# Transposing 64 rows in place of 128 for the half-filled expert blocks of a mixture-of-experts encoder layer

## The reference

```python
def expert_block(args):
    xb, e = args
    gt = jnp.minimum(xb @ w_gate[e] + b_gate[e], SWIGLU_LIMIT)
    up = jnp.clip(xb @ w_up[e] + b_up[e], -SWIGLU_LIMIT, SWIGLU_LIMIT)
    hdn = (up + 1.0) * (gt * jax.nn.sigmoid(SWIGLU_ALPHA * gt))
    return hdn @ w_down[e] + b_down[e]
...
out = jax.ops.segment_sum(y * gate, tok_pad, num_segments=T)
return rmsnorm(h + out, g_final)
```

## Time and profile before

| | |
|---|---|
| time, three runs | 1344.82, 1348.51 (median), 1349.32 us |
| profiled execution | 1343.44 us, of which the span of its instructions is 1341.7 us |
| TensorE busy | 1270.3 us (95%) |
| VectorE busy | 1230.4 us (92%) |
| ScalarE busy | 969.7 us (72%) |
| moved by DMA | 473.31 MB, 353 GB/s over the span |
| granted TensorE clock, mean | 0.981 |

### The profile page before, as it was taken

How to read it: one execution, slowest core, us unless ns; L and a number is a source line. 1 busy time by engine, 2 the same in 40 slices (tenths; PEclk the granted TensorE clock), 3 DMA queues, 4 the chain that set the end, 5 groups by cost and what they waited for, 6 DMA issues and landing times.

```text
span 1341.7 us, 17612 instructions
## 1 busy us (share of the span) xinstructions
PE 1270.3 (95%) x5771; PEld 1012.1 (75%) x5771; DVE 1230.4 (92%) x1014; ACT 969.7 (72%) x784; POOL 174.0 (13%) x165
## 2 busy tenths in 40 slices
PE   4998889878999999999999999999999999999997
PEld 3876767756878777787877777778787777777775
DVE  6798966699999999999999999999999999999998
ACT  3241665438797979797888888887979787879762
POOL 3010000012020101010101101020101010101243
PEclk9998989979999999999999999999999999999998
DMA  8964401489999999999999999999999999999985
GB/s 286 386 183 127 157 1 38 154 312 417 383 400 414 411 419 410 420 409 420 409 421 409 419 409 420 408 422 409 410 419 411 418 411 419 413 418 422 413 319 166
DMA packets 85574, 473.31 MB, mean 353 GB/s; under 512 B 11899, under 2 KB 12198, under 8 KB 36390
## 3 DMA queue, kind: packets, MB, share of 16 engines
q1 hardware_dynamic: 73838, 437.07, 81.0%
q0 software_dynamic: 6560, 18.90, 4.6%
q10 hardware_dynamic: 5144, 16.93, 3.3%
HBM read 447.72 MB, written 29.33 MB: 356 GB/s over the span
## 4 chain that ended last, share of the span: by engine, by line
PE 67%; DVE 14%; DMA 7%; ACT 6%; issue 3%; SPq 1%; ACTq 1%; POOL 0%; DVEq 0%
PE pair L1938 14%; PE pair L1939 13%; PE pair L1940 13%; DMA w_raw<-in_w_up 6%; PE pair L1954 5%; PE pair L1955 5%; DVE w_low L1285 5%; ACT w_high L831 3%; DVE area_m L1135 3%; PE pair L1925 2%; PE pair L1973 2%; PE pair L1952 1%; PE pair L1716 1%; PE pair L1717 1%; PE pair L1718 1%
## 5 line engine op out<-in xcount | busy, mean ns | idle before, releaser
L1285 DVE TENSOR_TENSOR w_low<-w_raw,w_high 128x2048 fp32r<-128x2048 f32 x380 | 838.4, 2247 | 40.9 <-ACT w_high L831 39.7
L831 ACT CAST w_high<-w_raw 128x2048 fp32r<-128x2048 f32 x380 | 702.9, 1878 | 170.4 <-PE pair L1940 117.1
L1938 PE MATMUL pair<-w_high,xT_high 128*128 128x512 f32 x528 | 211.4, 400 | 0.0
L1939 PE MATMUL pair<-w_low,xT_high 128*128 128x512 f32 x528 | 206.7, 392 | 0.0
L1940 PE MATMUL pair<-w_high,xT_low 128*128 128x512 f32 x528 | 206.1, 390 | 0.0
L1954 PE MATMUL pair<-w_high,xS 128*128 128x512 f32 x450 | 183.3, 407 | 0.1
L1955 PE MATMUL pair<-w_low,xS 128*128 128x512 f32 x450 | 175.8, 391 | 0.0
L1938 PEld LDWEIGHTS pair<-w_high,xT_high 128*128 128x128 f32 x528 | 99.2, 188 | 31.9 <-issue 11.4
L1940 PEld LDWEIGHTS pair<-w_high,xT_low 128*128 128x128 f32 x528 | 99.2, 188 | 21.5
L1939 PEld LDWEIGHTS pair<-w_low,xT_high 128*128 128x128 f32 x528 | 99.2, 188 | 19.1
L1938 PE MATMUL pair<-w_high,hT_high 128*128 128x512 f32 x256 | 102.0, 399 | 10.9 <-DVE w_low L1285 10.9
(11 more groups left out here) (355 smaller groups left out, 1793.5 us busy)
## 6 DMA issues: line engine op xcount, KB each, us to landing
w_raw<-in_w_gate SPq DMA_DIRECT2D x128, 1024.0 KB, 15.4
w_raw<-in_w_up SPq DMA_DIRECT2D x128, 1024.0 KB, 16.7
w_raw<-in_w_down SPq DMA_DIRECT2D x128, 1024.0 KB, 16.6
ring<-in_w_in SPq DMA_DIRECT2D x5, 2048.0 KB, 17.8
y_rows<-area_t SPq DMA_DIRECT2D x1, 8704.0 KB, 37.0
y_rows<-area_m ACTq DMA_DIRECT2D x15, 512.0 KB, 7.8
ring<-in_w_out SPq DMA_DIRECT2D x2, 2048.0 KB, 8.0
y_rows<-area_t SPq DMA_DIRECT2D x1, 3840.0 KB, 12.5
```

Of the source, the lines that this page charges most:

```text
L831: s.copy(w_high[:, i % HIGH_RING, raw:], w_raw[i][:, raw:]).then_inc(high_ready, 1)
L1285: v.tensor_tensor(w_low[i][:, raw:], w_raw[i][:, raw:], w_high[:, i % HIGH_RING, raw:].bitcast(F32), ALU.subtract).then_inc(low_ready, 1)
L1938: t.matmul(to[half], tok_high, hi, start=(opens and kk == 0), stop=False)
L1939: t.matmul(to[half], tok_high, lo, start=False, stop=False)
```

## The change

`transpose_x` and `transpose_h` get a parameter `first_row`. With 64, the first transpose of the set is as before and the other seven take the rows 64 to 127 alone: 64 x 128 stationary, 64 moving columns, written to the columns 64 to 127 of each 128. It is given for the x and the h of the small blocks 1, 3, ..., 29. That is 15 sets of x and 15 of h, so 210 instructions. All else, with the readers of the results, stays as it is.

```diff
-            def transpose_x(b):
+            def transpose_x(b, first_row=0):
                 pe.wait_ge(xg_loaded, 16 * (b + 1))
                 for k in range(KD):
-                    last = t.transpose(bank[6 + k // 4][:, (k % 4) * CAP:(k % 4 + 1) * CAP], xg[0:CAP, k::KD],
-                                       ident[0:CAP, 0:CAP])
+                    r = first_row if k else 0
+                    last = t.transpose(bank[6 + k // 4][:, (k % 4) * CAP + r:(k % 4 + 1) * CAP], xg[r:CAP, k::KD],
+                                       ident[r:CAP, r:CAP])
                 last.then_inc(xg_transposed, 1)
...
-            def transpose_h(b):
+            def transpose_h(b, first_row=0):
                 pe.wait_ge(h_tok_ready, b + 1)
                 for k in range(KD):
-                    last = t.transpose(bank[6 + k // 4][:, (k % 4) * CAP:(k % 4 + 1) * CAP], h_tok[:, k::KD],
-                                       ident[0:CAP, 0:CAP])
+                    r = first_row if k else 0
+                    last = t.transpose(bank[6 + k // 4][:, (k % 4) * CAP + r:(k % 4 + 1) * CAP], h_tok[r:, k::KD],
+                                       ident[r:CAP, r:CAP])
                 last.then_inc(h_transposed, 1)
...
-            def pe_odd(j):
+            def pe_odd(j, next_from=SMALL):
                 base = PIECES * j + 8
-                gate(j + 1, base, turn=j)
+                gate(j + 1, base, turn=j, turn_from=SMALL)
                 up(j + 1, base + UP)
                 pe.wait_ge(hT_low_ready, j + 1)
-                transpose_x(j + 2)
+                transpose_x(j + 2, next_from)
                 down(j, base + DOWN, small=True)
...
-            up(0, UP, high=x0T_high, low=x0T_low, between=lambda: transpose_x(1))
+            up(0, UP, high=x0T_high, low=x0T_low, between=lambda: transpose_x(1, SMALL))
...
-            pe_odd(N_EXPERTS - 3)
+            pe_odd(N_EXPERTS - 3, next_from=0)
```

More of the change, by code:

```diff
@@ L1975, in _, with gate @@
             G_TO, U_TO, D_TO = ([bank[i][0:CAP, :], bank[i + 1][0:CAP, :]] for i in (0, 2, 4))
-            def gate(b, base, turn=None, high=xT_high, low=xT_low, between=None, fold_down=None, small=False):
+            def gate(b, base, turn=None, high=xT_high, low=xT_low, between=None, fold_down=None, small=False, turn_from=0):
                 pe.wait_ge(sel_in_ready, b + 1)
@@ L1994, in gate @@
                     if i == 1 and turn is not None:
-                        transpose_h(turn)
+                        transpose_h(turn, turn_from)
                     if i == 1 and between is not None:
```

## The result

The changed kernel takes 1350.62 us (median of 12 runs, 1348.37 to 1356.17), the kernel before 1345.80 us in its 12 runs (1343.40 to 1349.89). The ratio is 1.0042, with a 95% interval of 1.0027 to 1.0057: slower by 0.4%, a little more than what can be told from no change.

What follows compares the result with a forecast made beforehand. TensorE bounds early pairs, weight transfers late ones. 28 sets at 0.28 us add 7.8, hidden by 8.8 to spare in a median run; 1348.5 plus 0.3 for the last set and 0.5 for meeting lines gives 1349.3 us, range 1345 to 1353.5.

Steps and rivals of the forecast that it cites:

- The bound: Experts' pairs of passes: TensorE sets the pace until the prefetch is used up near 957 us, then weight transfers do.
- TensorE's line: Pace of the experts' passes if TensorE's work alone set it: 63.23 us a pair.
- the transfers' line: Pace that weight loads allow the experts' passes: one pair in 64.2 us, taking over near 957 us.
- What a set costs: Eight transposes of a small block's x or h: 0.88 us before, 1.15 to 1.16 changed, so +0.28 us.
- The sign that the prediction gave: In the profile after, "issue" idle on PEld at L1918 and L1925, 0.1 to 0.2 us twice a set.
- The time to spare in the profiled execution: At the experts' last copy TensorE is 3.7 us ahead of transfers, hiding that much of 7.8 us added.
- To the median: Lays the 5.1 us from profiled execution to median to the transfer rate, giving TensorE 8.8 us to spare.
- the prediction's first rival: Spread of run times is not the transfers'; only 3.7 us spare in every run, so 1352.9 us, +0.33%; chance 0.25.
- The 0.5 us that it added for two lines that meet: In late pairs, TensorE and transfers within a microsecond wait now for one, now the other: about 0.5 us more.
- That a set costs nothing more: 64-row loads 0.063 us apart, or no drain for half-size transposes; time stays 1348.5 to 1348.6 us; chance 0.18.
- that the visit costs 0.41: Switching to 64 rows and back costs 0.41 us a set or above: 1351.6 us, or 1356.7; chance 0.10.
- the side on which fewer moving columns pay: Halved moving columns shorten transposes by 0.19 us a set and transfers only echo TensorE: 1342.9 us; chance 0.05.

Runs made afterwards that it cites:

- every second transpose: In each of the 30 sets, transposes k = 1, 3, 5, 7 take 64 rows and the others 128; against the kernel before, ratio 1.0254.
- x sets alone: Only the 15 x sets have seven 64-row transposes, h sets as in the kernel before; against that kernel, ratio 1.0007.

## Why the prediction was right and where it was wrong

**The bound: right.** TensorE's line and the transfers' line are in both profiles of before, with the same handover; taking TensorE's work away moved the handover forward and not the end. In the changed kernel the chain was to show no w_up transfer, TensorE's extra wait of late pairs was to be gone, and landing times were to rise by half a microsecond a pair. There is no such transfer, the idle time of the late pair is 63.90 - 63.50 = 0.4 us where it was 64.32 - 62.89 = 1.4, and landing times go from 9.7 to 15.5 us over 11 pairs.

**What a set costs: right in mechanism, a term too small.** The way in was put at 0.29 us from matmul to matmul and is 0.31 (0.20 to the load, 0.11 from there), the way out at 0.26 and is 0.26. Most of what was off is the middle, six distances put at 0.10 us and read off a single pair of loads; they are 0.108. Together +0.34 and not +0.28 a set; the pairs show 0.70 for two. 28 sets make 28 x 0.35 = 9.8 us in place of 7.8. The sentence on the Trainium skill's page "TensorE: Matmul & The Clock Gate", section "LDWEIGHTS (loading the stationary operand)", would have given 0.107 for the distance and +0.32, nearer to what was measured. That a load's time goes by the columns and not by the rows agrees as far as the rows go: loads of 64 rows and 128 columns follow each other by 0.108 us, those of 128 rows by 0.11; no run here changes the columns. The drain that the Trainium skill's page "TensorEngine Tiling (Array Packing)" names under "Key Properties" fits what is paid for, here 0.20 us in and about 0.15 us out; the traces show loads that begin late, not what TensorE does meanwhile. The sign that the prediction gave, "issue" idle of 0.1 to 0.2 us twice a set, stands once a set, on the way in, with 0.24; the way out shows only in the distance of the loads.

**The time to spare in the profiled execution: right.** With the measured cost, 9.8 - 3.7 = 6.1 us were to be added between the first and the last copy. It is (1220.6 - 323.8) - (1213.6 - 322.8) = 6.0. The set behind them, 0.3, is not seen: from there to the end are 127.8 us (1348.4 - 1220.6) against 128.1. The x set of block 1 costs nothing, as said: with four visits in it, in the kernel with every second transpose, the first copy is at 322.8 as before. The 3.7 itself is 3.8 from start to start, since the row at 387.95 of the earlier trace rows is the last 0.90 us of a copy that takes 1.00.

**The step "To the median": wrong, and it decided the forecast's side.** It laid the 5.1 us between the profiled execution and the median of three runs to the rate of the transfers, and so gave TensorE 8.8 us to spare in a median run. The profiles put the spread in the attention, ahead of the experts, where it goes with TensorE's clock, and it shifts both lines; 3.7 us are all there is to spare. This was the prediction's first rival, held at 0.25, and it is the one that happened: with the set's cost as forecast it gives 4.4 us or 0.33%, with the measured one 28 x 0.35 - 3.7 + 0.35 = 6.4 us or 0.48%, beside a measured 0.42% (0.27 to 0.57). That the forecast's absolute time is near is partly luck: its base of 1348.5 us was 2.7 above the median of twelve runs. The 0.5 us that it added for two lines that meet did not arise in the changed kernel, where no pair waits for transfers; with the x sets alone it was 0.8.

**The other rivals.** That a set costs nothing more is out by the timeline, that the visit costs 0.41 as with wide matmuls around it is near (0.34), and the side on which fewer moving columns pay is out twice: 64 moving columns do not bring the transposes closer together, and less work does not bring the end forward.

**Open:** what sets the 0.20 and 0.15 us of a change of rows, and why the attention is granted 0.80, 0.84 or 0.91 of the clock from one execution to the next, with the same code there.

## What to carry to other kernels

Before an instruction is made smaller, ask what its distance to the next one is made of. For float32 transposes in a stream it stayed at 0.11 us with 64 or 128 rows and with 52, 64 or 128 moving columns. That leaves the load of 128 stationary columns, which all of them have; no run was made with fewer. The change from 128 to 64 rows and back cost 0.34 us whether one or seven instructions lay in between; so 64-row work is put together, beside 64-row work that is there already.

Where two lines of supply and use run close, as 63.23 and 64.2 us a pair here, work out by how much each is ahead at the end: an addition counts only for what exceeds it, and a saving on the side that waits counts for nothing. And a spread of the times is no evidence on either line until two profiles show which stretch it lies in.

## What was not expected of the hardware

The attention stretch, 75 us of the span, was granted 0.80, 0.84, 0.89 or 0.91 of the clock in executions of the same code, and the first `bias_gu` copy came between 322.8 and 330.2 us. From there to the end the two executions of before agreed within 0.3 us (1018.9 and 1018.6), and those of the changed kernel within 0.2 (1024.6 and 1024.4).
